# One comparison builds the one-hots of four tokens, the scalar engine weights them, and the table of u tiles is dealt out anew

## The reference, cut to what matters

```
s = einsum('nhpd,hpkd->nhpk', q, subkeys)
sv, si = top_k(s, 16)
cand = (sv[:, :, 0, :, None] + sv[:, :, 1, None, :]).reshape(n, 8, 256)
cv, ci = top_k(cand, 16)
e1 = take_along_axis(si[:, :, 0, :], ci // 16, axis=-1)
e2 = take_along_axis(si[:, :, 1, :], ci % 16, axis=-1)
gates = softmax(cv, axis=-1)
a = gelu(einsum('cd,ckd->ck', x, u_tab[experts]))
y = einsum('ck,ckd->cd', gates * a, v_tab[experts])
```

## Time and profile before

| | |
|---|---|
| three runs | 5181.9, 5190.64, 5194.68 us; median 5190.64 |
| profiled execution | span 5194.2 us from the first to the last instruction; no other time of it is listed |
| PE, matmul | 5060.3 us busy (97%) |
| PE, weight loads | 4206.2 us (81%) |
| DVE | 3318.4 us (64%) |
| ACT | 1738.8 us (33%) |
| POOL | 1353.8 us (26%) |
| mean granted TensorE clock | 0.983 of full |

### The profile page before, as it was taken

The page is one execution under the profiler, slowest core; times in us unless marked ns, Lnnn a source line. Parts: engine busy times, 40 slices in busy tenths (PEclk is TensorE's granted clock), DMA queues, the critical chain, the costliest instruction groups (busy, mean ns, idle before and its releaser), DMA issues.

```text
span 5194.2 us, 70128 instructions
## 1 busy us (share of the span) xinstructions
PE 5060.3 (97%) x26242; PEld 4206.2 (81%) x26242; DVE 3318.4 (64%) x7279; ACT 1738.8 (33%) x2726; POOL 1353.8 (26%) x906
## 2 busy tenths in 40 slices
PE   7999999999999999999999999999999999999999
PEld 4666899788888888888876668999888888888887
DVE  2865432149899876666648654320798899666666
ACT  3344432333333332222233443323333333322222
POOL 1300233234434421111113002332444434111111
PEclk9989999999999999999999899999999999999999
DMA  7100122556787788888820001222577787888886
GB/s 273 44 26 1 46 75 66 207 205 225 259 283 256 242 313 292 290 290 290 288 76 29 26 1 51 76 68 78 194 267 240 260 287 240 318 289 290 290 290 221
DMA packets 349901, 982.06 MB, mean 189 GB/s; under 512 B 31648, under 2 KB 101408, under 8 KB 346272
## 3 DMA queue, kind: packets, MB, share of 16 engines
q1 hardware_dynamic: 216000, 553.19, 32.1%
q0 software_dynamic: 74880, 276.86, 15.4%
q10 hardware_dynamic: 58720, 148.04, 7.3%
HBM read 829.43 MB, written 148.54 MB: 188 GB/s over the span
## 4 chain that ended last, share of the span: by engine, by line
PE 85%; DVE 7%; DMA 2%; ACT 2%; issue 1%; DVEq 1%; POOL 0%; ACTq 0%; POOLq 0%; SPq 0%
PE PS L943 27%; PE PS L900 24%; PE PS L513 18%; PE PS L924 4%; PE PS L656 3%; PE PS L684 3%; DVE AR L1354 2%; PE PS L668 1%; PE PS L626 1%; PE PS L502 1%; PE PS L887 1%; DVE AR L1375 1%; DVE SM L1393 1%; DMA gates_by_expert<-AR 1%; DMA WR<-in_wq 1%
## 5 line engine op out<-in xcount | busy, mean ns | idle before, releaser
L943 PE MATMUL PS<-HB,VR 128*128 128x512 f32 x6144 | 1393.2, 389 | 3.2 <-DVE HB L1671 3.2
L943 PEld LDWEIGHTS PS<-HB,VR 128*128 128x128 f32 x6144 | 1153.2, 188 | 244.0 <-issue 4.8
L900 PE MATMUL PS<-HR,UR 128*128 128x512 f32 x4128 | 1008.0, 398 | 0.0
L513 PE MATMUL PS<-HR,UR 128*128 128x320 f32 (+1 forms) x5952 | 914.0, 312 | 17.9 <-POOL UR L1714 9.6
L513 PEld LDWEIGHTS PS<-HR,UR 128*128 128x128 f32 x5952 | 884.1, 189 | 49.0 <-issue 32.4
L900 PEld LDWEIGHTS PS<-HR,UR 128*128 128x128 f32 x4128 | 764.4, 189 | 165.9
L1714 POOL TENSOR_TENSOR UR<-WR,UR 128x1024 fp32r<-128x1024 f32 x228 | 571.8, 2508 | 797.5 <-ACT UR L1093 511.5
L1658 DVE TENSOR_TENSOR VR<-HT,VR 128x1024 fp32r<-128x1024 f32 x256 | 313.8, 1226 | 455.7 <-ACT VR L1279 373.1
L1279 ACT CAST VR<-HT 128x1024 fp32r<-128x1024 f32 x256 | 268.8, 1050 | 961.1 <-PE PS L943 958.6
L900 PE MATMUL PS<-HR 128*128 128x512 f32 x2016 | 486.7, 394 | 0.0
L900 PEld LDWEIGHTS PS<-HR 128*128 128x128 f32 x2016 | 372.1, 188 | 73.6
(11 more groups left out here) (210 smaller groups left out, 6263.9 us busy)
## 6 DMA issues: line engine op xcount, KB each, us to landing
WR<-in_uT SPq DMA_DIRECT2D x256, 512.0 KB
HT<-in_vtab SPq DMA_DIRECT2D x256, 512.0 KB
activations<-AR ACTq DMA_DIRECT2D x256, 256.0 KB
gates_by_expert<-AR ACTq DMA_DIRECT2D x128, 512.0 KB, 3.4
HW<-activations SPq DMA_DIRECT2D x256, 256.0 KB
WR<-gates_by_expert SPq DMA_DIRECT2D x64, 1024.0 KB
AR<-in_ada SPq DMA_DIRECT2D x40, 1024.0 KB, 7.5
WR<-in_wgate SPq DMA_DIRECT2D x64, 640.0 KB, 3.9
```

Source lines behind the costliest of these rows:

```text
L513: last = pe.matmul(out(lo, hi), part(w, c), whole(h, c, lo, hi), start=start and i == 0, stop=stop and i == 2)
L900: last = pe.matmul(bank(n % 2), u_part(n, w)[:, c, :], HR[:, h, c, 0:LAT], start=c == 0 and i == 0, stop=c == DC - 1 and i == 2)
L943: last = pe.matmul(bank(d), VR[:, m % 4, w, P * d:P * d + P], HB[:, (m + 1) % 3, h, :], start=m == 0 and i == 0, stop=m == E1 - 1 and i == 2)
```

## The change

- The candidates of a head are no longer all 256 pairs of ranks but 64: rank 0 of the first set with 16 of the second, ranks 1 to 3 with 8, ranks 4 to 7 with 4, ranks 8 to 15 with 1 (`PAIR_ROWS`). A pair outside of these has 16 better ones. The place in the list of 64 is turned back to two ranks by comparisons with where each row starts.
- The one-hots of four tokens, both sides, are one comparison over 1024 columns; the weight is a second step, four scalings in place on ACT (`weigh_one_hots`), signalled by a semaphore of its own (`one_hots_weighted`), for which PE now waits.
- `AHEAD` is 11, so `PER_TILE` is 27 and `AFTER` is 9.
- `keep_busy(7, 8)` is gone, and ACT's last casts are put at the last three u tiles again.

```diff
-AHEAD, BESIDE = 12, 16
+AHEAD, BESIDE = 11, 16
+PAIR_ROWS = ((0, 1, 16), (1, 3, 8), (4, 4, 4), (8, 8, 1))
+PAIR_AT = [0, 16, 40, 56]
...
-                            last = pe.matmul(bank(2 + m % 2)[:, P * k:P * k + P], HOT[:, m % 2, 2 * k, :], HOT[:, m % 2, 2 * k + 1, :],
+                            last = pe.matmul(bank(2 + m % 2)[:, P * k:P * k + P], HOT[:, m % 2, 1, k, :], HOT[:, m % 2, 0, k, :],
...
-                keep_busy(7, 8)
...
+                def weigh_one_hots(t, m):
+                    act.wait_ge(hot_made, l * PICKS + BATCHES * t + m + 1)
+                    for k in range(4):
+                        last = nc.scalar.activation(HOT[:, m % 2, 0, k, :], HOT[:, m % 2, 0, k, :], ACT.Identity,
+                                                    scale=EWT[:, 2, 4 * m + k:4 * m + k + 1])
+                    last.then_inc(hot_ready, 1)
...
+                    weigh_one_hots(t, 0)
                     for m in range(BATCHES):
...
+                        if m + 1 < BATCHES:
+                            weigh_one_hots(t, m + 1)
                         act.wait_ge(gmm_done, l * PICKS + BATCHES * t + m + 1)
...
-                gelu(E1 - AFTER + 1)
+                for n in range(E1 - AFTER + 1, E1 - 2):
+                    gelu(n)
                 act.wait_ge(gd_out[0], 16 * PIECES * LTILES * (l + 1))
                 high_v(0)
-                gelu(E1 - AFTER + 2)
+                gelu(E1 - 2)
                 high_v(1)
-                gelu(E1 - AFTER + 3)
+                gelu(E1 - 1)
                 high_v(2)
...
-                    nc.vector.tensor_tensor(m1, V4[:, :, 0, :].unsqueeze(3).broadcast_to(all4),
-                                            V4[:, :, 1, :].unsqueeze(2).broadcast_to(all4), ALU.add)
+                    for at, (a, n, w) in zip(PAIR_AT, PAIR_ROWS):
+                        nc.vector.tensor_tensor(c1[:, :, at:at + n * w].rearrange("p h (a b) -> p h a b", a=n),
+                                                V4[:, :, 0, a:a + n].unsqueeze(3).broadcast_to([P, PH, n, w]),
+                                                V4[:, :, 1, 0:w].unsqueeze(2).broadcast_to([P, PH, n, w]), ALU.add)
...
-                        for k in range(4):
-                            tok = slice(4 * m + k, 4 * m + k + 1)
-                            nc.vector.tensor_scalar(HOT[:, m % 2, 2 * k, :], iota, EWT[:, 1, tok], None, ALU.is_equal)
-                            last = nc.vector.tensor_scalar(HOT[:, m % 2, 2 * k + 1, :], iota, EWT[:, 0, tok], EWT[:, 2, tok],
-                                                           ALU.is_equal, ALU.mult)
-                        last.then_inc(hot_ready, 1)
+                        nc.vector.tensor_tensor(HOT[:, m % 2], EWT[:, 0:2, 4 * m:4 * m + 4].unsqueeze(3).broadcast_to([P, 2, 4, P]),
+                                                iota.unsqueeze(1).unsqueeze(1).broadcast_to([P, 2, 4, P]),
+                                                ALU.is_equal).then_inc(hot_made, 1)
                         dot(g)
                         if m % 2 == 0 and m >= 2:
-                            low_u(n0 + 13 + m // 2)
+                            low_u(n0 + AHEAD + 1 + m // 2)
```

More of the change, by code:

```diff
@@ L95 @@
 C_EPS = C_I16 + 16
-C_ALL = C_EPS + 1
+C_ROW = C_EPS + 1
+C_ALL = C_ROW + 16
 TRIG = 6 * LAT
+PAIR_ROWS = ((0, 1, 16), (1, 3, 8), (4, 4, 4), (8, 8, 1))
+PAIR_AT = [0, 16, 40, 56]
+PAIRS = 64
 class Arena:
@@ L208, in build @@
         eps = CN[:, C_EPS:C_EPS + 1]
+        row_starts = CN[:, C_ROW:C_ROW + 16]
         MODT = PF[:, 1024:1024 + 2 * N_ADA]
@@ L261, in build @@
         UG = p_.take(2, D)
-        HOT = p_.take(2, 8, P)
+        HOT = p_.take(2, 8, P).rearrange("p b (s k) e -> p b s k e", s=2)
         V1, I1, I1F = p_.take(SUB, TOPK), p_.take(SUB, TOPK), p_.take(SUB, TOPK)
         CV, CI, CM, CE = p_.take(PH, TOPK), p_.take(PH, TOPK), p_.take(PH, TOPK), p_.take(PH, TOPK)
-        CA, CB, CAF, CBF = p_.take(PH, TOPK), p_.take(PH, TOPK), p_.take(PH, TOPK), p_.take(PH, TOPK)
+        STEP, CB, CAF, CBF = p_.take(PH, TOPK), p_.take(PH, TOPK), p_.take(PH, TOPK), p_.take(PH, TOPK)
         EW = p_.take(3, P)
@@ L331, in build @@
             "sub_scores", "sub_scores_out", "chosen_minus_max", "chosen_exp", "choice_ready"))
-        tr_ready, ewt_ready, hot_ready, gmm_done, g_evac = (sem(n) for n in (
-            "choice_turned", "choice_t_out", "one_hots", "gates_spread", "gates_copied"))
+        tr_ready, ewt_ready, hot_made, hot_ready, gmm_done, g_evac = (sem(n) for n in (
+            "choice_turned", "choice_t_out", "one_hots", "one_hots_weighted", "gates_spread", "gates_copied"))
         gd_out = [sem(f"gates_stored{k}") for k in range(2)]
@@ L1548, in _ @@
                     low_u(n)
-                I1U, CIU, CAU, CBU = (x.bitcast(U32) for x in (I1, CI, CA, CB))
+                I1U, CIU, CBU = (x.bitcast(U32) for x in (I1, CI, CB))
+                FIFTEEN = SM[:, 128:144].bitcast(U32)
+                nc.vector.memset(FIFTEEN, 15)
                 s1, s2 = (x.rearrange("p (b k) -> p b k", b=SUB) for x in (S1, S2))
-                c1, c2 = (x.rearrange("p (h k) -> p h k", h=PH) for x in (S1, S2))
+                c1, c2 = (x[:, 0:PH * PAIRS].rearrange("p (h k) -> p h k", h=PH) for x in (S1, S2))
                 m1, m2 = (x.rearrange("p (h s k) -> p h s k", h=PH, s=TOPK) for x in (S1, S2))
@@ L1596, in choose @@
                     dve.drain()
-                    nc.vector.tensor_copy(CAF, CAU)
+                    nc.vector.tensor_tensor(m1, CAF.unsqueeze(3).broadcast_to(all4),
+                                            row_starts.unsqueeze(1).unsqueeze(1).broadcast_to(all4), ALU.is_ge)
+                    nc.vector.tensor_scalar(CBF, CAF, float(PAIR_AT[1]), None, ALU.is_ge)
+                    dve.drain()
+                    nc.vector.tensor_tensor(m2, m1, STEP.unsqueeze(2).broadcast_to(all4), ALU.mult)
@@ new lines, in choose @@
+                    nc.vector.scalar_tensor_tensor(CBF, CAF, float(PAIR_AT[2]), CBF, ALU.is_ge, ALU.add)
+                    nc.vector.tensor_scalar(CAF, CAF, float(PAIR_AT[3]), 2.0, ALU.is_ge, ALU.mult)
+                    dve.drain()
+                    nc.vector.reduce_sum(ew[:, 0, :].rearrange("p (h k) -> p h k", h=PH), m2, AX.X)
+                    nc.vector.tensor_tensor(CBU, CBF, CAF, ALU.add)
+                    dve.drain()
+                    nc.vector.tensor_tensor(CBU, FIFTEEN.unsqueeze(1).broadcast_to([P, PH, TOPK]), CBU, ALU.logical_shift_right)
@@ L1598, in choose @@
+                    dve.drain()
+                    nc.vector.tensor_tensor(CBU, CIU, CBU, ALU.bitwise_and)
+                    dve.drain()
                     nc.vector.tensor_copy(CBF, CBU)
                     dve.drain()
-                    for side, place in enumerate((CAF, CBF)):
-                        nc.vector.tensor_tensor(m1, place.unsqueeze(3).broadcast_to(all4),
-                                                iota16.unsqueeze(1).unsqueeze(1).broadcast_to(all4), ALU.is_equal)
-                        dve.drain()
-                        nc.vector.tensor_tensor(m2, m1, F4[:, :, side, :].unsqueeze(2).broadcast_to(all4), ALU.mult)
-                        dve.drain()
-                        nc.vector.reduce_sum(ew[:, side, :].rearrange("p (h k) -> p h k", h=PH), m2, AX.X)
-                        dve.drain()
+                    nc.vector.tensor_tensor(m1, CBF.unsqueeze(3).broadcast_to(all4),
+                                            iota16.unsqueeze(1).unsqueeze(1).broadcast_to(all4), ALU.is_equal)
@@ L1609, in choose @@
+                    dve.drain()
+                    nc.vector.tensor_tensor(m2, m1, F4[:, :, 1, :].unsqueeze(2).broadcast_to(all4), ALU.mult)
+                    dve.drain()
+                    nc.vector.reduce_sum(ew[:, 1, :].rearrange("p (h k) -> p h k", h=PH), m2, AX.X)
+                    dve.drain()
                     dve.wait_ge(ce_ready, l * TILES + (i + 1))
@@ L1851, in make_consts @@
     c[:, C_EPS] = EPS
+    c[:, C_ROW:C_ROW + 16] = [at + i * w for at, (_, n, w) in zip(PAIR_AT, PAIR_ROWS) for i in range(n)]
     return c
```

7 lines of the change are left out of this document (4 added, 3 removed).

## The result

The changed kernel takes 5227.65 us (median of 4 runs, 5223.24 to 5233.52) against 5186.97 us (4 runs, 5181.9 to 5194.68): a ratio of 1.0079, interval 1.0064 to 1.0095, or +33 to +49 us. The forecast was 5219 us, slower by 28.6 us; measured are 41. The profiled execution has a span of 5225.6 us, 31.4 more than before.

A forecast was written before the change was run, and what follows sets the result against it. PE, busy 97% of the span, was taken to bound the kernel. Terms -10.0 - 3.5 + 23.1 + 19.0 = +28.6 us gave 5219 us (+0.55%); the likeliest case's own range was 5210 to 5233.

The forecast's parts named there:

- start of a stage: Spread stage starts: PE stands 3.0 us for ACT's scalings, queued behind gelu and cast, eight times; +23.1 us.
- end of u: Between the last u tile and v: PE's hole shrinks from 8.6 to 3.6 us in each layer; -10.0 us.
- The picks: First transposes of each layer: DVE's choice ends 13.5 us earlier, so PE's wait of 1.74 us goes; -3.5 us.
- DVE's one-hots: Spread stage: one comparison taken at 1.22 us relieves DVE, hidden under PE either way; no change in time.
- ACT's scaling: Steady spread stage: four scalings take 1.28 us and fit into 1.77 us; no change in time.
- The clock: Behind PE's new waits of 2.9 and 3.6 us the clock halves, costing 1.9 us ten times; +19 us.
- Rival 1: The clock holds behind PE's new waits: +9.6 us, 5200 us, no change; chance 0.15.
- Rivals 2 and 3: Steady spread stage: ACT or DVE overruns, 5258 us, chance 0.12; or one-hots had held PE, under 5175 us, chance 0.06.
- Rival 4: Stage starts: the stall is covered since scalings slip in earlier; 5181 us, no change; chance 0.05.

The follow-up runs named there:

- experiment 2: The changed kernel with ACT's casts of the first two gated tiles ahead of the last gelu of u: 5216.79 us, ratio 1.0049 to before.
- experiment 6: The changed kernel with POOL making the u tiles' low parts for a quarter of the columns only: 5211.68 us, ratio 1.0032 to before.
- experiment 5: The kernel before with only the choice among 64 pairs a head in place of 256: 5192.47 us, ratio 0.9996 to before.
- experiment 7: The changed kernel with `AHEAD` = 12 and the idle matmuls ahead of v again: 5218.64 us, ratio 1.0043 to before.
- experiment 4: The kernel before with only the new one-hots and their scaling on ACT: 5213.88 us, ratio 1.0047 to before.
- Experiment 1: The changed kernel with the scalings of a stage's first batch ahead of the last whole tile's gelu on ACT: 5199.71 us, ratio 1.0021 to before.
- experiment 9: The kernel before with 16 unused columns of constants, buffers behind them 64 bytes further on: 5195.44 us, ratio 1.0011 to before.

## Why the prediction was right, and which step failed

The direction was right, and so were the terms for the start of a stage and the end of u. The size came out low: +28.6 us forecast, +41 (33 to 49) measured. One step failed and one term was missing, and both left time out. Step by step:

- **End of u, -10.0.** Forecast 3.6 us left of 8.6; measured 3.47 in both layers, -10.3. The row of the wait names the step (DVE's subtraction), and experiment 2 shows the cause.
- **The picks, -3.5: this step failed.** It said that DVE would end 13.5 us earlier than before, and took eight small steps "at about 0.2 each" as cancelled by the smaller sum. The saving on pairs and sum, 7.9 + 1.6 = 9.5 us, is what the rows show. But three of the small steps are held by POOL and take 2.43, 2.51 and 1.15 us, so the choice is 2.6 us shorter, not 7.9. DVE hands the picks over 9.5 us earlier than before (1216.24 for 1225.71), PE arrives 12.1 us earlier (1211.93 for 1224.06), and the wait grew from 1.74 to 4.39: +5.3 us for -3.5. That the choice is held is shown by experiment 6, its net saving by experiment 5; with `AHEAD` = 12, where PE arrives later, the same choice leaves no wait (experiments 5 and 7). The rows of before had it: L1604 took 3.52 us on average over 2048 columns, where one alone takes 2.29.
- **DVE's one-hots, nothing.** A comparison takes 1.22 us in a steady batch, as taken; the first of a stage takes 3.17 in six of eight stages.
- **ACT's scaling, nothing in the steady stage.** Four take 1.28 us, as estimated, one 0.395. PE's pace stays (experiment 4). The profile's 4.86 and 5.77 us for ACT and DVE in 7.30 are the forecast's 5 and 6.
- **Start of a stage, +23.1.** 3.0 us forecast, 2.79 measured, eight times; from the transposes to the first product 2.93 more than before, 8 x 2.93 = +23.4. Experiment 1 takes 18.8 us of the waits away by one move in a queue.
- **The clock, +19.** Right in sum, 20.6, by luck, and wrong in detail: not 1.9 ten times, but 1.7 at six of the eight starts, 3.4 at one of the two ends, and 3.4 at each of the two waits for the picks, which should not have been there. The ten places that it priced cost 13.7. Where a wait near 2.8 us costs the clock and where not, no run tells; in experiment 7 the same wait cost 3.4, 1.7 and twice nothing in the first layer.
- **Missing: where the buffers lie.** The table of row starts moves every buffer behind the constants by 64 bytes, some +7 us (experiments 5, 7, 9). The whole diff shows it as a change of `C_ALL` and `AF`, and I priced it at nothing by not naming it. That the place changes PE's pace is shown; the 7 us are worked out from stages and stretches, and the total of experiment 9 doesn't show them by itself.

The measured terms are -10.3 + 5.3 + 23.4 + 20.6 + 7 = +46 us, against +33 to +49 by the runs. The two profiled spans differ by 31.4 only. Of the 14.6 us between them, most is that the execution of before lost 46.1 us to half clock in the second layer ahead of its u part, which the change doesn't touch, and the changed one 34.1; over the fourteen profiles it is 29.0 to 47.8 there.

Rival 1 (the clock holds) holds for two of eight starts. Rivals 2 and 3 fell with experiment 4. Rival 4 fell: the stall stands at all eight starts, and it takes another order to cover most of it (experiment 1).

Open: why the place of the buffers changes PE's pace, and which distance is best; only three places were tried. Whether `AHEAD` = 11 or 12 is better once the waits are gone was not tried.

## What to carry to other kernels

When a step moves to another engine, price its place in that engine's queue before its length: here 1.28 us of scalings were free 248 times and cost 2.93 us wherever a gelu of unfinished work stood ahead of them, and 1.7 us of clock more in six of those eight; moving one line took most of that back. Where POOL runs two-operand steps beside DVE, as here, don't count small DVE steps at their free price; each can be held for what is left of POOL's. And a change of a buffer's size is a change of the time: time a version with the size alone.
